# Scan and output projection of a two-block forward pass: the residual addition of a product group moved ahead of a scan step's outputs, and a finer wait for the split tiles

## The chip, the cores and the metric

One NeuronCore of a Trainium2 chip runs the whole program in one launch. The metric is the device time of that core in microseconds (us); the time of a kernel is the median over its runs.

## What is computed

Two blocks over one sequence of 512 tokens and width 1024, all in float32. The first block projects the input, runs a dilated window attention and a Mamba-2 scan, and joins both by one output projection:

```python
y = ssd_chunked(...)                       # 4 chunks of 128 tokens, 16 heads in 2 groups
y = y + d_skip[:, None] * xs_h
y_ssm = rms_norm(y * silu(z_ssm), ssm_norm_g)
mix = concatenate([y_att, y_ssm], axis=-1)             # 2048 columns
out = einsum('bse,ed->bsd', mix, w_out)                # 2048 x 1024 weights
x = layer_norm(alpha * x + out, ln_g, ln_b)
```

In a chunk the scan needs, for each group g of 8 heads: the products C.B (one 128x128 tile), the decay matrix of each head (an exponential of differences of sums), the masked product of both, that matrix times x*dt (y_diag), C times the running state (y_off), and the new state. The second block (a gated delta rule mixer with its own projections) follows and is not touched.

## The kernel before

The program has four phases on one core: the first projections, the attention, `scan_and_output` (from about 388 to 562 us of the span) and `second_mixer` (from there to the end). Only `scan_and_output` is concerned. Each engine has its own instruction list, written out by hand, and the lists meet only in semaphores.

**The work of the phase.** There are 8 scan steps (`STEPS`, step s is chunk s // 2 and head group s % 2). Beside them runs the output projection for the attention half of `mix`, in 8 groups (`GROUPS`). Group i makes one tile of 128 tokens by 512 columns: it sums 8 row tiles of weights, each as three products of split numbers (`three_products`, lines 129 to 131: high by high, high by low, low by high), so 24 matmuls into PSUM bank ACC (bank 7). VectorE then adds the tile, scaled by a factor of its row, to `resid` (`add`, line 1257) and increments `added`. There is only one such bank, so group i + 1 may not start before `added` has reached i + 1. The weights come in 8 units of 4 row tiles; of each unit ScalarE makes the high part (`round`, line 280) and VectorE the low part (`rest`, line 284).

**TensorE's order.** For s = 0 to 6: `ahead_of(s + 1)`, `group(s)`, `outputs(s)`; after the loop `outputs(7)` and `group(7)`. (`ahead_of(0)` and `ahead_of(1)` come before the loop.) `ahead_of` transposes the next step's inputs (L942, L949), makes C.B (L950) and the sums for the decays (L956). `outputs` makes y_off (L967), the state's part (L974) and eight y_diag products (L978); it waits for `z_ok` of the step before, since VectorE must have read the banks.

**VectorE's order.** In iteration s: `steps_of(s + 1)` (x times dt, L1203, L1207, and the masked C.B, L1214) and `masked(s + 1)` (L1220), then `outputs(s)` (L1229 to L1253; the last, L1253, increments `z_ok`), then `add_group(s)` (L1257). At s = 3 `rest(2)` stands ahead of `outputs(3)`, and `rest(3)` between `outputs(3)` and `add_group(3)`. `steps_of(0)`, `masked(0)`, `steps_of(1)` and `masked(1)` come before the loop. ScalarE's `ahead_of(s + 1)` (L1074, L1079, L1083) waits for `z_ok` of step s - 1, then copies the transposed inputs, on which the next `steps_of` waits. GpSimd makes the sums' inputs (L1146) and a skip term (L1153).

**The second half of the projection.** After group 7, TensorE transposes the first four column tiles of the scan's result (`turn`, L934); ScalarE writes each one's high part (`high`, L1067), VectorE its low part (`low`, L1194, increments `m_lo_ok`). Then come four token tiles of unit 4 in banks 4 to 7, each of 12 products. Ahead of all four stands one wait for the first four low tiles:

```python
            pe.wait_ge(w.lo_ready, 5)
            pe.wait_ge(m_lo_ok, KT + 4)
            for t in range(TT):
                if t == TT - 1:
                    pe.wait_ge(added, GROUPS)
                mm = unit_tile(4, t, 4 + t, True, False)
                if t == 1:
                    for e in range(KT + 4, MT):
                        turn(e)
```

Units 5 to 7 follow, and VectorE normalises the rows of `resid` as the token tiles are finished. The next phase starts when all engines have left this one.

Of the kernel before, what the change touches and what calls it, by code (L numbers as in the profile page):

```python
# [15 lines left out]
KT = D_MODEL // P  # L16
# [59 lines left out]
class Phase(ExitStack):  # L76
# [14 lines left out]
    def sem(self, name):  # L91
        s = self.enter_context(self.nc.semaphore(f"{self.name}_{name}"))
        Phase.used.append(s.num)
        return s
# [32 lines left out]
def three_products(nc, out, w_hi, w_lo, x_hi, x_lo, first, last):  # L127

    nc.tensor.matmul(out, w_hi, x_hi, start=first, stop=False, skip_group_check=True)  # L129
    nc.tensor.matmul(out, w_hi, x_lo, start=False, stop=False, skip_group_check=True)  # L130
    return nc.tensor.matmul(out, w_lo, x_hi, start=False, stop=last, skip_group_check=True)  # L131
# [685 lines left out]
def scan_and_output(nc, a, ahead, wba, wba_in, mix_in, raw, att_f, m_g, masks, small, resid, row_f, tok, xbc, dt, adt, modc):  # L817
# [8 lines left out]
    STEPS = G * TT  # L826
# [7 lines left out]
    with ctx:  # L834
# [35 lines left out]
        turned, m_hi_ok, m_lo_ok = sem("turned"), sem("m_hi_ok"), sem("m_lo_ok")  # L870
# [14 lines left out]
        def head_row(values):  # L885

            return values.unsqueeze(2).broadcast_to([P, HPG, HD])

        def heads_of(g):
            return slice(g * HPG, (g + 1) * HPG)  # L890
# [4 lines left out]
        def slot_of(e):  # L895

            return e % KT
# [27 lines left out]
        def _(pe):  # L925
            pe.sem_inc(w.units_used, 2)

            def turn(e):

                bank = 7 - e % 4 if e < KT else e % 4  # L930
                if e % KT >= 4:
                    pe.wait_ge(m_lo_ok, e - 3)
                for t in range(TT):
                    tr = nc.tensor.transpose(ps[:, bank, t * P:(t + 1) * P], tok[:, t, e * P:(e + 1) * P], ident)  # L934
                tr.then_inc(turned, 1)
# [42 lines left out]
                    mm = nc.tensor.matmul(ps_yd[:, h, :], E[:, g, h, :], xdt[:, g, h, :], start=True, stop=True)  # L978
                mm.then_inc(yd_made, 1)

            def unit_tile(u, t, bank, first, last):
                s, k0 = u % 2, OUT_UNITS[u][1]
                rows = slice(t * P, (t + 1) * P)
                for kk in range(HALF):
                    k = slot_of(k0 + kk)
                    mm = three_products(nc, ps[:, bank, :], m_hi[:, k, rows], m_lo[:, k, rows],
                                        w.hi[s][:, kk, :], w.lo[s][:, kk, :], first and kk == 0, last and kk == HALF - 1)
                return mm

            def group(i):  # L990
                n, t = divmod(i, TT)
                if i:
                    pe.wait_ge(added, i)
                for x in range(2):
                    u = 2 * n + x
                    pe.wait_ge(w.lo_ready, u + 1)
                    if i == 0:

                        pe.wait_ge(m_lo_ok, KT if x else HALF + 1)
                    mm = unit_tile(u, t, ACC, x == 0, x == 1)  # L1000
                    if t == TT - 1:
                        mm.then_inc(w.units_used, 1)
                    elif x:
                        mm.then_inc(acc_made, 1)

            flat = adt[:].rearrange("p c h -> p (c h)")
            for n, mask in enumerate((upper, below, ones)):
                mm = nc.tensor.matmul(ps_c[:, n, 0:TT * SSM_HEADS], mask, flat, start=True, stop=True)
# [17 lines left out]
            for e in range(KT, KT + 4):  # L1026
                turn(e)
            pe.wait_ge(w.lo_ready, 5)
            pe.wait_ge(m_lo_ok, KT + 4)
            for t in range(TT):  # L1030
                if t == TT - 1:
                    pe.wait_ge(added, GROUPS)
                mm = unit_tile(4, t, 4 + t, True, False)
                if t == 1:
                    for e in range(KT + 4, MT):
                        turn(e)
# [3 lines left out]
            for t in range(TT):  # L1040
                mm = unit_tile(5, t, 4 + t, False, True)
                if t < TT - 1:
                    mm.then_inc(acc_made, 1)
# [11 lines left out]
            for j in range(3 * KT):  # L1055
                mm = nc.tensor.matmul(ps[:, 4, j:j + P], mod_acc[:, j * P:(j + 1) * P], ones, start=True, stop=True)
# [128 lines left out]
        def _(dve):  # L1185
            own = Own(dve, own_s)

            def rest(u):
                w.rest(nc.vector, dve, u % 2, u // 2)
# [7 lines left out]
            def steps_of(s):  # L1197
                c, g = divmod(s, G)

                dve.wait_ge(xs_out, s + 1)  # L1200
                if s >= G:
                    dve.wait_ge(yd_made, s - 1)
                ins = nc.vector.tensor_tensor(xdt[:, g], ps_x, head_row(dt[:, c, heads_of(g)]), ALU.mult)  # L1203
                if s < FIRST:
                    if s >= G:
                        dve.wait_ge(st_made, s - 1)
                    ins = nc.vector.tensor_tensor(xdte[:, g], ps_x, head_row(dte[:, c, heads_of(g)]), ALU.mult)  # L1207
                ins.then_inc(x_read, 1)
                dve.wait_ge(cb_made, s + 1)
                if s < FIRST:  # L1210
                    dve.wait_ge(b_out, s + 1)
                if s >= G:
                    dve.wait_ge(m_ok, s - 1)
                nc.vector.tensor_tensor(cb[:, g, :], ps_c[:, 1, :], upper, ALU.mult).then_inc(cb_ok, 1)  # L1214

            def masked(s):
                g = s % G
                dve.wait_ge(cb_ok, s + 1)
                dve.wait_ge(e_ok, s + 1)
                nc.vector.tensor_tensor(E[:, g], E[:, g], cb[:, g, :].unsqueeze(1).broadcast_to([P, HPG, P]), ALU.mult)\  # L1220
                    .then_inc(m_ok, 1)

            def outputs(s):
                c, g = divmod(s, G)
                if s:
                    dve.wait_ge(z_ok, s)
                if c:
                    dve.wait_ge(yo_made, s - 1)
                    own.did(nc.vector.tensor_tensor(y[:], ps_yo, head_row(decays[:, 0, c, heads_of(g)]), ALU.mult))  # L1229
                    y_step = own.n  # L1230
                    if s < FIRST:
                        dve.wait_ge(st_ok, s - 1)
                        own.did(nc.vector.tensor_tensor(state[:, g], state[:, g], head_row(decays[:, 2, c, heads_of(g)]), ALU.mult))
                        state_step = own.n
                dve.wait_ge(yd_made, s + 1)
                if c:
                    own.wait(y_step)
                    own.did(nc.vector.tensor_tensor(y[:], ps_yd, y[:], ALU.add))
                    y_step = own.n
                if s < FIRST:  # L1240
                    dve.wait_ge(st_made, s + 1)
                    if c:
                        own.wait(state_step)
                        nc.vector.tensor_tensor(state[:, g], ps_st, state[:, g], ALU.add).then_inc(st_ok, 1)
                    else:
                        nc.vector.tensor_copy(state[:, g], ps_st).then_inc(st_ok, 1)
                dve.wait_ge(xskip_ok, s + 1)
                if c:
                    own.wait(y_step)
                own.did(nc.vector.tensor_tensor(y[:], y[:] if c else ps_yd, xs_tok[:, g], ALU.add))  # L1250
                z = tok[:, c, D_MODEL + g * GW:D_MODEL + (g + 1) * GW].rearrange("p (h e) -> p h e", e=HD)
                own.wait()
                nc.vector.tensor_tensor(z, y[:], z, ALU.mult).then_inc(z_ok, 1)  # L1253

            def add(half, t, bank, factor):
                x = resid[:, t, half * COLS:(half + 1) * COLS]
                nc.vector.scalar_tensor_tensor(out=x, in0=ps[:, bank, :], scalar=factor[:, t:t + 1], in1=x,  # L1257
                                               op0=ALU.mult, op1=ALU.add).then_inc(added, 1)

            def add_group(i):  # L1260
                n, t = divmod(i, TT)
                if i == 0:
                    dve.wait_ge(factor_ok, 1)
                    dve.wait_ge(rows_in, 64)
                if t < TT - 1:
                    dve.wait_ge(acc_made, (TT - 1) * n + t + 1)
                else:
                    dve.wait_ge(w.units_used, 2 + 2 * (n + 1))
                add(n, t, ACC, att_f)
# [17 lines left out]
            for s in range(STEPS):  # L1287
                if 1 <= s < STEPS - 1:
                    steps_of(s + 1)
                    masked(s + 1)  # L1290
                if s == TT - 1:
                    rest(2)
                outputs(s)
                if s == TT - 1:
                    rest(3)
                if s < STEPS - 1:
                    add_group(s)
            rest(4)
            for e in range(KT, KT + 4):
                low(e)  # L1300
# [1428 lines left out]
```

## Time and profile before

| what | value |
|---|---|
| time, median of 3 runs | 1202.41 us (1197.02 to 1203.72) |
| the profiled execution's own time | 1204.67 us |
| its span, first to last instruction | 1202.8 us |
| granted TensorE clock, mean over the span | 0.972 of full |
| TensorE matmul busy, share of the span | 93% |
| VectorE, ScalarE, GpSimd busy | 59%, 39%, 18% |

How to read it: the times of a row are in microseconds, "mean ns" is the mean length of one instruction in nanoseconds. PE is TensorE's matmuls, PEld its weight loads, which overlap them, DVE is VectorE, ACT ScalarE, POOL GpSimd; an engine name with a q is its queue. Matmuls are pipelined and their ends are modelled, so two neighbours overlap in the records. "<-" in square brackets names the work that ended an idle time. The clock is given as a fraction: 1.00 is 2.4 GHz, 0.50 is 1.2 GHz, and a number between them is a stretch with some of each.

### The profile page before, as it was taken

To read this page: it belongs to the slowest core of one execution; us is meant where nothing else is said; L and a number is where in the kernel's file an instruction comes from. 1 tells how busy PE (TensorE), PEld (TensorE's weight loads), DVE (VectorE), ACT (ScalarE), POOL (GpSimd) and SP (SyncE) were. 2 spreads that over 40 slices of the span, in tenths; PEclk is the share of its full clock that TensorE was granted. 3 is DMA by queue.
4 is the path that set the end of the run, shared out by engine and by line. 5 is a ranking of instruction groups with operands and counts; after the bars stand their busy time and mean duration, and the time that the engine had idled before them with its cause. 6 is when DMAs were issued, how large, how long until landed. Compare 5 with 4: busy or idle time off the path is not lost.

```text
span 1202.8 us, 15175 instructions
## 1 busy us (share of the span) xinstructions
PE 1123.1 (93%) x5878; PEld 930.5 (77%) x5878; DVE 705.3 (59%) x1144; ACT 465.8 (39%) x853; POOL 218.9 (18%) x155
## 2 busy tenths in 40 slices
PE   6999999999899998896999999999999889999887
PEld 3888888888698766685687888788798867788776
DVE  3344446521465875447558667566545667756778
ACT  3233134421565531222343333476244446244421
POOL 0001000000000421006100000033433233444044
PEclk9999999999899999898999999999999979999989
DMA  7277424330410410222144354432211212121401
GB/s 276 81 251 255 164 85 143 99 128 0 132 54 17 173 36 35 96 97 87 68 140 141 127 189 140 140 118 93 71 53 54 88 37 88 35 71 36 158 1 71
DMA packets 58307, 124.04 MB, mean 103 GB/s; under 512 B 5760, under 2 KB 5888, under 8 KB 58112
## 3 DMA queue, kind: packets, MB, share of 16 engines
q1 hardware_dynamic: 55792, 110.22, 27.2%
q0 software_dynamic: 2304, 12.58, 2.8%
q8 instruction: 44, 0.72, 0.2%
q10 hardware_dynamic: 144, 0.33, 0.1%
q14 instruction: 23, 0.19, 0.1%
HBM read 108.96 MB, written 14.16 MB: 102 GB/s over the span
## 4 chain that ended last, share of the span: by engine, by line
PE 39%; DVE 8%; issue 2%; POOL 2%; ACT 2%; DMA 0%; DVEq 0%; POOLq 0%; ACTq 0%
PE mixer_ps L129 8%; PE mixer_ps L130 8%; PE mixer_ps L131 8%; PE mixer_ps L1833 3%; PE mixer_ps L1831 3%; DVE z L2580 2%; PE mixer_ps L1859 2%; DVE resid L240 1%; PE mixer_ps L1873 1%; PE mixer_ps L1864 1%; PE mixer_ps L1835 1%; POOL mixer_w_lo L284 1%; PE mixer_ps L1794 1%; PE mixer_ps L1845 1%; PE mixer_ps L1805 1%
## 5 line engine op out<-in xcount | busy, mean ns | idle before, releaser
L284 DVE TENSOR_TENSOR projections_w_lo<-raw,projections_w_hi 128x2048 fp32r<-128x2048 f32 x26 | 59.6, 2293 | 146.1 <-ACT projections_w_hi L280 146.1
L280 ACT ACTIVATE projections_w_hi<-raw 128x2048 fp32r<-128x2048 f32 x26 | 49.8, 1914 | 158.8 <-PE projections_ps L131 157.2
L284 DVE TENSOR_TENSOR mixer_w_lo<-raw,mixer_w_hi 128x2048 fp32r<-128x2048 f32 x21 | 48.1, 2289 | 71.1 <-ACT mixer_w_hi L280 60.3
L129 PE MATMUL projections_ps<-projections_x_hi,projections_w_hi 128*128 128x512 f32 x224 | 87.3, 390 | 0.0
L131 PE MATMUL projections_ps<-projections_x_hi,projections_w_lo 128*128 128x512 f32 x224 | 87.1, 389 | 0.0
L130 PE MATMUL projections_ps<-projections_x_lo,projections_w_hi 128*128 128x512 f32 x224 | 87.1, 389 | 0.0
L129 PE MATMUL projections_ps<-projections_w_hi,projections_x_hi 128*128 128x512 f32 x192 | 74.7, 389 | 0.0
L130 PE MATMUL projections_ps<-projections_w_lo,projections_x_hi 128*128 128x512 f32 x192 | 74.7, 389 | 0.0
L131 PE MATMUL projections_ps<-projections_w_hi,projections_x_lo 128*128 128x512 f32 x192 | 74.7, 389 | 0.0
L240 DVE SCALAR_TENSOR_TENSOR resid<-resid,mixer_cw 128x512 f32<-128x512 f32 x96 | 64.9, 745 | 0.0
L129 PE MATMUL output_ps<-output_w_hi,output_m_hi 128*128 128x512 f32 x128 | 53.1, 415 | 9.3 <-DVE resid L1257 6.5
L129 PE MATMUL mixer_ps<-mixer_w_hi,mixer_ha_hi 128*128 128x512 f32 x128 | 55.9, 437 | 5.9 <-ACT z L2065 2.6
L2526 DVE COPY_PREDICATED mixer_space<-mixer_masks,mixer_ps 128x512 f32<-128x512 int32 x48 | 35.4, 737 | 43.4 <-PE mixer_ps L1833 42.9
L2296 POOL TENSOR_TENSOR mixer_es<-masks,mixer_gsel 128x1024 f32<-128x1024 f32 x8 | 15.5, 1939 | 230.9 <-DVE mixer_bsel L2448 197.0
L129 PE MATMUL mixer_ps<-mixer_w_hi,mixer_hb_hi 128*128 128x512 f32 x128 | 52.1, 407 | 1.5 <-POOL mixer_w_lo L1548 1.4
L130 PE MATMUL output_ps<-output_w_lo,output_m_hi 128*128 128x512 f32 x128 | 51.8, 404 | 0.0
L280 ACT ACTIVATE mixer_w_hi<-raw 128x2048 fp32r<-128x2048 f32 x18 | 34.3, 1908 | 44.5 <-PE mixer_ps L131 44.5
L131 PE MATMUL output_ps<-output_w_hi,output_m_lo 128*128 128x512 f32 x128 | 51.4, 401 | 0.0
L130 PE MATMUL mixer_ps<-mixer_w_lo,mixer_ha_hi 128*128 128x512 f32 x128 | 51.3, 401 | 0.0
L131 PE MATMUL mixer_ps<-mixer_w_hi,mixer_ha_lo 128*128 128x512 f32 x128 | 51.1, 399 | 0.0
L129 PE MATMUL mixer_ps<-mixer_ha_hi,mixer_w_hi 128*128 128x512 f32 x128 | 50.0, 391 | 0.7 <-DVE mixer_w_lo L284 0.7
L1833 PE MATMUL mixer_ps<-mixer_space 128*128 128x128 f32 x384 | 50.4, 275 | 0.0
(309 smaller groups left out, 2860.9 us busy)
## 6 DMA issues: line engine op xcount, KB each, us to landing
raw<-in_w_in SPq DMA_DIRECT2D x26, 1024.0 KB, 5.1
raw<-in_gdn_w_in SPq DMA_DIRECT2D x24, 1024.0 KB, 5.1
tok<-in_ada_w POOLq DMA_DIRECT2D x16, 768.0 KB, 6.4
raw<-in_w_out SPq DMA_DIRECT2D x8, 1024.0 KB, 5.8
qkv_kept<-mixer_ring SPq DMA_DIRECT2D x8, 1024.0 KB, 4.3
mixer_st<-qkv_kept SPq DMA_DIRECT2D x32, 256.0 KB, 3.0
raw<-in_gdn_w_out SPq DMA_DIRECT2D x8, 1024.0 KB, 5.3
resid<-in_att_bias SPq DMA_DIRECT2D x16, 256.0 KB, 2.7
```

The lines of the kernel that those rows point to most:

```text
L129: nc.tensor.matmul(out, w_hi, x_hi, start=first, stop=False, skip_group_check=True)
L130: nc.tensor.matmul(out, w_hi, x_lo, start=False, stop=False, skip_group_check=True)
L131: return nc.tensor.matmul(out, w_lo, x_hi, start=False, stop=last, skip_group_check=True)
L240: ins = nc.vector.scalar_tensor_tensor(out=acc, in0=src, scalar=tap, in1=acc, op0=ALU.mult, op1=ALU.add)
L280: self.nc.scalar.activation(self.hi[s][:], self.raw[s][:], ACT.Copy).then_inc(self.hi_ready, 1)
L284: engine.tensor_tensor(self.lo[s][:], self.raw[s][:], self.hi[s][:], ALU.subtract)\
L1831: mm = nc.tensor.matmul(out, C[:, 8 * j + m, :], T[:, m, :], start=True, stop=True)
L1833: mm = nc.tensor.matmul(out, V[:, m, :], U[j % 2][:, m, :], start=True, stop=True)
L1859: mm = nc.tensor.matmul(psW[:, h, :], U[slot][:, 4 * h + c, :], rhs, start=True, stop=True)
L2296: nc.gpsimd.tensor_tensor(steps, upper.unsqueeze(1).broadcast_to([P, 8, P]), gs.unsqueeze(2).broadcast_to([P, 8, P]), ALU.mult).then_inc(s ...
L2526: nc.vector.copy_predicated(U[j % 2][:, 4 * grp:4 * grp + 4, :], level.unsqueeze(1).broadcast_to([P, 4, P]), psZ[:, grp, :].rearrange("p ( ...
L2580: nc.vector.scalar_tensor_tensor(out=zz, in0=O[j % 2][:, h, c, :], scalar=rs[:, j % 2, h, c:c + 1], in1=zz, op0=ALU.mult, op1=ALU.mult).th ...
```

## The change

In VectorE's loop `add_group(s)` moves from behind `outputs(s)` (and behind `rest(3)` at s = 3) to ahead of `outputs(s)` (and behind `rest(2)`). In TensorE's list the one wait for four low tiles ahead of unit 4 goes, and the first token tile (t = 0) waits ahead of each of its four weight row tiles for the low tile that it needs. No arithmetic, transfer or buffer is added or removed.

```diff
-            def unit_tile(u, t, bank, first, last):
+            def unit_tile(u, t, bank, first, last, lows=False):
                 s, k0 = u % 2, OUT_UNITS[u][1]
                 rows = slice(t * P, (t + 1) * P)
                 for kk in range(HALF):
+                    if lows:
+                        pe.wait_ge(m_lo_ok, k0 + kk + 1)
                     k = slot_of(k0 + kk)
                     mm = three_products(nc, ps[:, bank, :], m_hi[:, k, rows], m_lo[:, k, rows],
                                         w.hi[s][:, kk, :], w.lo[s][:, kk, :], first and kk == 0, last and kk == HALF - 1)
...
             pe.wait_ge(w.lo_ready, 5)
-            pe.wait_ge(m_lo_ok, KT + 4)
             for t in range(TT):
                 if t == TT - 1:
                     pe.wait_ge(added, GROUPS)
-                mm = unit_tile(4, t, 4 + t, True, False)
+                mm = unit_tile(4, t, 4 + t, True, False, t == 0)
...
                 if s == TT - 1:
                     rest(2)
+                if s < STEPS - 1:
+
+                    add_group(s)
                 outputs(s)
                 if s == TT - 1:
                     rest(3)
-                if s < STEPS - 1:
-                    add_group(s)
             rest(4)
```

## Rows read from the trace of the kernel before

**Rows 1.** Waits from 402 to 562 us: in total, times, longest, in us.
```profile
PE output_ps L129 <- DVE resid L1257: 6.5, 6, 3.1
...
PE output_ps L129 <- DVE output_m_lo L1194: 2.7, 1, 2.7
...
PE output_ps L967 <- DVE tok L1253: 2.3, 1, 2.3
```
**Rows 2.** Timeline of PE, before the steps and in steps 2 to 4: start, length, line.
```profile
395.02 1.88 PE L956 MATMUL output_ps<-output_steps_in,masks 128*128 128x512 f32 x4
396.74 1.91 PE L934 MATMUL output_ps<-masks,tok 128*128 128x128 f32 x16
...
430.98 1.02 PE L967 MATMUL output_ps<-output_state,xbc 128*128 128x512 f32 x2
...
437.96 0.50 PE L129 MATMUL output_ps<-output_w_hi,output_m_hi 128*128 128x512 f32 x1 [0.87 <-DVE resid L1257]
...
443.54 1.02 PE L967 MATMUL output_ps<-output_state,xbc 128*128 128x512 f32 x2
...
447.76 1.88 PE L956 MATMUL output_ps<-output_steps_in,masks 128*128 128x512 f32 x4
452.71 0.63 PE L129 MATMUL output_ps<-output_w_hi,output_m_hi 128*128 128x512 f32 x1 [3.07 <-DVE resid L1257]
...
459.90 0.59 PE L967 MATMUL output_ps<-output_state,xbc 128*128 128x512 f32 x1
```
**Rows 3.** Timeline of DVE, steps 2 and 3.
```profile
432.11 0.69 DVE L1229 TENSOR_TENSOR output_y<-output_ps,output_decays 128x512 f32<-128x512 f32 x1 [2.67 <-PE output_ps L967]
...
436.55 0.69 DVE L1253 TENSOR_TENSOR tok<-output_y,tok 128x512 f32<-128x512 f32 x1
437.16 0.74 DVE L1257 SCALAR_TENSOR_TENSOR resid<-output_ps,att_f,resid 128x512 f32<-128x512 f32 x1
437.96 0.69 DVE L1203 TENSOR_TENSOR output_xdt<-output_ps,dt 128x512 f32<-128x512 f32 x1
...
439.49 2.51 DVE L1220 TENSOR_TENSOR output_E<-output_E,output_cb 128x1024 f32<-128x1024 f32 x1
443.02 2.29 DVE L284 TENSOR_TENSOR output_w_lo<-raw,output_w_hi 128x2048 fp32r<-128x2048 f32 x1 [1.03 <-ACT output_w_hi L280]
...
447.18 0.69 DVE L1238 TENSOR_TENSOR output_y<-output_ps,output_y 128x512 f32<-128x512 f32 x1 [0.67 <-PE output_ps L978]
...
449.71 2.28 DVE L284 TENSOR_TENSOR output_w_lo<-raw,output_w_hi 128x2048 fp32r<-128x2048 f32 x1
451.91 0.74 DVE L1257 SCALAR_TENSOR_TENSOR resid<-output_ps,att_f,resid 128x512 f32<-128x512 f32 x1
```
**Rows 4.** Timeline of ACT and POOL around steps 2 and 3.
```profile
437.34 0.60 ACT L1074 ACTIVATE output_xs_tok<-output_ps 128x512 f32<-128x512 f32 x1 [9.83 <-DVE tok L1253]
...
438.01 1.05 POOL L1153 TENSOR_TENSOR output_xs_tok<-output_xs_tok,small 128x512 f32<-128x512 f32 x1 [9.65 <-ACT output_xs_tok L1074]
...
450.56 2.33 POOL L1153 TENSOR_TENSOR output_xs_tok<-output_xs_tok,small 128x512 f32<-128x512 f32 x1 [9.65 <-ACT output_xs_tok L1074]
```
**Rows 5.** Stretches: us, busy time (x instructions) of each engine, PEclk, DMA share, GB/s.
```profile
452.70:456.20 3.50, 3.49 (x9) 2.71 (x10) 3.10 (x4) 0.00 (x0) 2.05 (x2) 0.53 0.77 277
...
490.10:494.90 4.80, 4.80 (x19) 3.92 (x19) 1.28 (x2) 0.00 (x0) 0.00 (x0) 0.54 0.43 134
...
506.10:513.30 7.20, 7.18 (x24) 5.69 (x25) 2.73 (x2) 0.31 (x1) 0.00 (x0) 0.76 0.66 240
```
**Rows 6.** Timeline of DVE and PE around the start of unit 4.
```profile
503.25 2.72 DVE L1194 SCALAR_TENSOR_TENSOR output_m_lo<-output_ps,mix_g,output_m_hi 128x512 fp32r<-128x512 f32 x4
...
501.56 1.91 PE L934 MATMUL output_ps<-masks,tok 128*128 128x128 f32 x16
506.12 0.47 PE L129 MATMUL output_ps<-output_w_hi,output_m_hi 128*128 128x512 f32 x1 [2.65 <-DVE output_m_lo L1194]
```
**Rows 7.** The second mixer as one stretch, columns as above.
```profile
562.00:1202.80 640.80, 596.14 (x3254) 501.06 (x3254) 418.92 (x676) 272.20 (x611) 166.28 (x97) 0.97 0.28 94
```

## The prediction

> **What bounds the kernel now.** I read the stretches first, then the waits, then the timeline of each engine. Over the phase TensorE has work nearly all the time, so what ends a wait of TensorE moves the end of the phase, and everything behind it. The table of waits shows three kinds that end on VectorE [rows 1]: the first product of a group waits for the residual addition (L1257) six times, 6.5 us in all, 3.1 us the longest; the first product of unit 4 waits 2.7 us for the low tiles; and the products of step 7 wait 2.3 us for step 6's result (L1253). The change aims at the first two and leaves the third.
>
> In the timeline group 3's last product is followed at 443.54 by the scan's products, and these by step 5's preparation, whose last four matmuls start at 447.76; then TensorE is idle until 452.71 [rows 2]. VectorE meanwhile works through the outputs, a weight unit's low part (449.71, 2.28 us) and only then the addition (451.91) [rows 3], although the tile was complete at about 443.5. So the addition is late only by its place in the list. For step 2 the same shape is smaller: the addition runs at 437.16, behind L1253.
>
> **The clock** belongs to the same bill. The granted clock is 0.53 in the 3.5 us behind the idle 3.1 us, 0.54 in the 4.8 us behind the idle 2.3 us, and 0.76 over the 7.2 us that follow the 2.7 us ahead of unit 4 [rows 1, 5]: stretches at the 1.2 GHz level, each behind an idle. The idle 0.87 us ahead of group 3 leaves no mark: its 24 products take 5.58 us [rows 2].
>
> **Part 1: the addition ahead of the outputs.** The wait for `added` goes if VectorE is at the addition when the group ends. Steps 1 to 6 have it so: for step 2 the group ends at 430.98 (start of L967), and VectorE is idle 2.67 us until 432.11, for L967's result [rows 2, 3]. The addition (0.74 us) fits between the tile's end, about 431.2, and 432.11, so the outputs and `z_ok` don't move. At step 3 VectorE is in `rest(2)` until 443.02 + 2.29 = 445.31 [rows 3], so the outputs start 0.7 us late; L1238 had been idle 0.67 us for TensorE and absorbs most of it. I take 0.2 us late for `rest(3)`. At step 0, whose outputs follow the first masks without a pause, nothing on VectorE covers the addition; its outputs come up to 0.74 us later, and what hides that is group 1 on TensorE, 5.6 us; without it step 1 would pay the 0.74.
>
> What is late next? TensorE's period is, group end to group end, 3.4 us of outputs, 2.5 of preparation and 5.5 of products, about 11.4. VectorE's period starts with the outputs, which end at 437.24, 6.26 us behind the group's end. Then ScalarE's copy (437.34 to 437.94) [rows 4] releases L1203 at 437.96, exactly where it starts today: the addition filled that hole and does not shorten the chain when it goes. The masked product ends at 439.49 + 2.51 = 442.00, 11.0 us behind the group's end [rows 3]. That is 0.4 us ahead of the next group's end, so VectorE just keeps up.
>
> The gain per wait: reported idle is 6.5 us over six waits [rows 1]. It counts from the modelled end of the last preparation matmul (1.88 us behind the first), while in an unbroken row the next instruction starts 1.72 us behind it (395.02 to 396.74 [rows 2]). That adds 6 x 0.16 = 1.0: **7.5 us**. Bounds: 6.5, and 7.5 if all of the pitch comes back. Group 4 also gets its clock back: it took 459.90 - 452.71 = 7.19 us, group 3 443.54 - 437.96 = 5.58 [rows 2]: **1.6 us**. The second half of group 4 needs `rest(3)`. That ended at 451.99, 8.45 us behind the group's end; group 4 would start 5.9 behind it and reach its second half at 5.9 + 2.8 = 8.7, and with 0.2 us of lateness `rest(3)` ends at 8.65 and hands over at about 8.8. I subtract **0.2** (bounds 0 and 1.0).
>
> The upper bound is where a GpSimd operation would start ahead of `rest(3)` and hold it up. The row: the GpSimd multiplication L1153 took 1.05 us at step 2 and 2.33 us at step 3, where it began at 450.56 inside `rest(3)` [rows 3, 4]. The Trainium skill, "SBUF — State Buffer", section "Who interferes with whom", says that the port which VectorE and GpSimd share is an exclusive lock: whoever starts first holds it for its whole instruction. By that rule the loser would be `rest(3)` only if L1153 came first, and the sum would be 11.7 in place of 12.5. L1153 waits for ScalarE's copy, which waits for the same L1253 that `rest(3)` follows directly, so both move together and I keep 0.2.
>
> **Part 2: a wait per low tile.** The four low tiles run from 503.25 to 505.97, so one is done each 0.66 us and the first at 503.25 + 0.74 = 503.99. TensorE started 0.15 us behind the last one (506.12) [rows 6]; now it starts at 504.14: **2.0 us**. Each row tile then takes three products at 0.23 (5.58 / 24), 0.7 us in all, as slow as the low tiles come, so no further wait. Four wait instructions come in where one was. Group 3 passes such a satisfied wait between its two units and keeps that pitch, so I cost them at zero (bounds 0 and 4 x 0.2, one exposed weight load each). Behind them on TensorE stands all of unit 4, for which ScalarE waits (rounding unit 6). Nothing is moved past the queues of SP or GpSimd; SP's loads wait for `lo_ready`, whose events hardly move. The addition of group 7, behind the low tiles, is needed only by the fourth token tile, some 8 us later.
>
> The clock: 24 products in 7.18 us [rows 5], while 24 at full clock take about 5.5: **1.6 us**, if the clock stays. What stays between group 7 and unit 4 are the 16 transposes (501.56 to 503.47) and an idle of 0.7 us instead of 2.65 [rows 6], nearer to the 0.87 us that did no harm than to the 2.3 that did. Bounds 0 and 1.6.
>
> **Sum**: 7.5 + 1.6 - 0.2 + 2.0 + 1.6 = **12.5 us**. Against the profiled execution's 1204.67 that is 1192.2. That execution stands 2.3 us above the median of the three runs, 1202.41; 1202.41 - 12.5 = 1189.9, and I give **1190.0**. The wait in front of step 7 stays: it hangs on VectorE's outputs of step 6, which move with TensorE's. The second mixer (640.8 us of the span [rows 7]) only starts earlier.
>
> **Rivals.**
> *The clock falls all the same at unit 4* or in group 4. For it: only a part of the 7.2 us behind the wait was slow (0.76 [rows 5]), so the fall is not tied to the wait alone, and small transposes come ahead of it. Against: the 0.87 us ahead of group 3 did nothing. Gain 12.5 - 1.6 = 10.9, with both 9.3: 1191.5 to 1193. Chance 0.2.
> *VectorE becomes the bound of the scan steps.* For it: the slack is only 0.4 us, and the list is in order, so a late mask now delays the addition, and with it the outputs. Against: L1229 and L1238 wait for TensorE anyway (1.1 and 0.7 us [rows 3]). Price up to 0.75 us, one addition, in each of six steps: gain 12.5 - 4.5 = 8.0, so 1194.4. Chance 0.1.
> *The waits on the addition are not what holds TensorE*: something else (the weight's low part, the next inputs) ends just behind it. Then only unit 4 gains, 2.0 to 3.6 us: about 1199.6, no change. For it: at step 3 `rest(3)` ends 0.08 us before the addition's start. Against: only the group's second half needs it, and the small waits have no such neighbour. Chance 0.08.
> *Slower: the clock's slow stretches in the second mixer grow.* The mechanism is that more of its short waits are followed by a stretch at 1.2 GHz, as the three above were, since everything there now starts 12 us earlier. One such stretch costs 1.6 us (7.19 - 5.58). It decides from 8 new stretches (12.5 / 1.6) and is slower by over 0.5% from 12: 1202.4 - 12.5 + 12 x 1.6 = 1209.1. The mixer's mean clock is 0.97 [rows 7], so it now holds 640.8 x 0.03 x 2 = 38 us at the lower level; 12 more of 3.5 us would double that. Chance 0.03.
>
> **How the numbers follow.** The forecast's case has 0.59, the clock at unit 4 or group 4 0.2, VectorE 0.1, no gain from the addition 0.08, slower 0.03. About 0.5%, 6 us, is what a measurement of this kernel can tell from no change (the three runs spread over 6.7 us). The low end takes the forecast's gain, 2.2 us more (4.8 x 0.46 [rows 5]) if the slow clock behind step 6 vanishes by the shift, and a median as far down as half of the runs' spread: 1184. The high end holds the first two rivals and most of the noise: 1198. Faster by over 0.5% is below 1196.4: 0.87; within: 0.10; slower: 0.03.
>
> **What would show it.** In the changed profile: no waits of L129 on L1257, or traces of 0.1 us; group 4 about 5.6 us long at clock 1.00; L1257 directly ahead of L1229 in VectorE's timeline and L1203 still 7.0 us behind the group's end; the wait on L1194 at about 0.7 us, with clock 1.00 behind it; the wait of 2.3 us on L1253 still there; the next phase about 12 us earlier. I would be wrong if L129 waited on L284 or L1220, if the same idle came back under another name ahead of L967, or if clock rows in the mixer fell.

## The result and the profile after

The changed kernel takes 1188.96 us (median; 1182.84 to 1190.15) against 1203.02 of the kernel before in the same comparison: ratio 0.9886, 95% interval 0.9846 to 0.9926, 14.1 us less. Measured again beside other kernels it was 1187.68 against 1202.69, ratio 0.9874 (0.9859 to 0.9889). The forecast was 1190.0, range 1184 to 1198, and 0.87 for a gain of over 0.5%.

In the changed file the lines from 990 on are one or two higher: L1257 is L1258, L1253 L1254, L1194 L1195, L1203 L1204, L1229 L1230. In some of the runs below they are shifted by one or two more (L1196 is L1194, L1255 is L1253).

The head of the page, then the waits from 402 to 550 us (in total, times, longest):

```profile
span 1188.4 us, 15175 instructions
```
```profile
DVE resid L1258 <- PE output_ps L131: 14.7, 10, 2.3
...
PE output_ps L967 <- DVE tok L1254: 2.3, 1, 2.3
...
PE output_ps L129 <- DVE output_m_lo L1195: 0.6, 1, 0.6
```

The six waits of L129 on the addition [rows 1] are gone without a trace. In their place VectorE waits for TensorE: ten waits of its additions for a finished tile, since VectorE is now there first. The wait ahead of unit 4 fell from 2.7 to 0.6 us, and the one for step 6's result is still 2.3.

TensorE's timeline, against [rows 2] and [rows 6]:

```profile
412.12 1.88 PE L956 MATMUL output_ps<-output_steps_in,masks 128*128 128x512 f32 x4
...
441.30 1.02 PE L967 MATMUL output_ps<-output_state,xbc 128*128 128x512 f32 x2
...
445.52 1.88 PE L956 MATMUL output_ps<-output_steps_in,masks 128*128 128x512 f32 x4
446.84 0.79 PE L129 MATMUL output_ps<-output_w_hi,output_m_hi 128*128 128x512 f32 x1
...
452.74 1.02 PE L967 MATMUL output_ps<-output_state,xbc 128*128 128x512 f32 x2
...
475.34 1.02 PE L967 MATMUL output_ps<-output_state,xbc 128*128 128x512 f32 x2
480.40 2.06 PE L967 MATMUL output_ps<-output_state,xbc 128*128 128x512 f32 x2 [2.31 <-DVE tok L1254]
...
493.51 1.91 PE L934 MATMUL output_ps<-masks,tok 128*128 128x128 f32 x16
496.06 0.47 PE L129 MATMUL output_ps<-output_w_hi,output_m_hi 128*128 128x512 f32 x1 [0.65 <-DVE output_m_lo L1195]
...
501.61 1.91 PE L934 MATMUL output_ps<-masks,tok 128*128 128x128 f32 x16
```

From the end of group 3 to the end of group 4 it is 452.74 - 441.30 = 11.44 us, where it was 459.90 - 443.54 = 16.36. L129 now starts inside L956's modelled length. VectorE's timeline, against [rows 3]:

```profile
430.07 0.75 DVE L1258 SCALAR_TENSOR_TENSOR resid<-output_ps,att_f,resid 128x512 f32<-128x512 f32 x1 [1.16 <-PE output_ps L131]
431.00 0.69 DVE L1230 TENSOR_TENSOR output_y<-output_ps,output_decays 128x512 f32<-128x512 f32 x1 [0.18 <-PE output_ps L967]
...
436.85 0.69 DVE L1204 TENSOR_TENSOR output_xdt<-output_ps,dt 128x512 f32<-128x512 f32 x1 [0.72 <-ACT output_xs_tok L1075]
...
447.48 2.29 DVE L284 TENSOR_TENSOR output_w_lo<-raw,output_w_hi 128x2048 fp32r<-128x2048 f32 x1
...
451.19 2.41 DVE L1221 TENSOR_TENSOR output_E<-output_E,output_cb 128x1024 f32<-128x1024 f32 x1
453.52 0.74 DVE L1258 SCALAR_TENSOR_TENSOR resid<-output_ps,att_f,resid 128x512 f32<-128x512 f32 x1
```

The addition lies in the hole ahead of L1230, and the hole that it leaves behind the outputs is now the wait of 0.72 us for ScalarE's copy. And the stretches of step 7 with group 7, and of the first two token tiles of unit 4, against [rows 5]:

```profile
480.40:485.50 5.10, 5.10 (x18) 4.07 (x19) 0.69 (x1) 0.00 (x0) 0.00 (x0) 0.50 0.35 104
485.50:493.50 8.00, 8.00 (x26) 6.34 (x26) 2.61 (x4) 1.92 (x1) 0.00 (x0) 0.68 0.32 133
...
496.00:501.60 5.60, 5.54 (x24) 4.56 (x25) 4.75 (x5) 2.38 (x2) 0.00 (x0) 1.00 0.60 187
```

**The bill of the first pair of profiles**, from TensorE's landmarks: group 6 ends 9.68 us earlier (485.02 to 475.34). Group 7 ends only 8.05 earlier (501.56 to 493.51), since step 7 and group 7 took 13.11 us at a lower clock, not 11.48. Unit 4 starts 10.06 earlier (506.12 to 496.06) and its first 24 products end 11.69 earlier (513.30 to 501.61). The second mixer's first VectorE operation moved from 562.26 to 550.57, again 11.69. The span fell by 14.4: the other 2.7 us came in the second mixer, 640.6 us from there to the end before and 637.8 after, where no instruction was changed. The granted clock of the mixer differs between the two profiles:

```profile
562.26:1202.83 640.57, 596.14 (x3254) 501.06 (x3254) 418.91 (x676) 272.20 (x611) 166.28 (x97) 0.97 0.28 94
...
550.57:1188.35 637.78, 590.80 (x3254) 496.91 (x3254) 418.87 (x676) 272.17 (x611) 167.77 (x97) 0.98 0.28 94
```

### The profile page after: what moved, and what is told of

Same layout as the page of the kernel before. It is cut to its first block, busy times and chain, and to the rows that moved or that the text cites. A ratio compares the mean times of both kernels' runs of the same rounds, so it can differ in the third digit from the quotient of the medians.

```text
span 1188.4 us, 15175 instructions
## 1 busy us (share of the span) xinstructions
PE 1115.0 (94%) x5878; PEld 926.3 (78%) x5878; DVE 706.2 (59%) x1144; ACT 465.9 (39%) x853; POOL 220.5 (19%) x155
## 4 chain that ended last, share of the span: by engine, by line
PE 37%; DVE 10%; issue 3%; ACT 2%; POOL 2%; DMA 0%; DVEq 0%; POOLq 0%; ACTq 0%
PE mixer_ps L129 7%; PE mixer_ps L131 7%; PE mixer_ps L130 7%; PE mixer_ps L1835 3%; PE mixer_ps L1833 3%; DVE z L2582 2%; PE mixer_ps L1861 2%; DVE resid L240 1%; PE mixer_ps L1875 1%; DVE resid L2660 1%; PE mixer_ps L1866 1%; PE mixer_ps L1837 1%; DVE mixer_ktok L2658 1%; POOL mixer_w_lo L284 1%; PE mixer_ps L1796 1%
## 5 line engine op out<-in xcount | busy, mean ns | idle before, releaser
L129 PE MATMUL projections_ps<-projections_x_hi,projections_w_hi 128*128 128x512 f32 x224 | 87.3, 390 | 0.0
L129 PE MATMUL projections_ps<-projections_w_hi,projections_x_hi 128*128 128x512 f32 x192 | 74.7, 389 | 0.0
L129 PE MATMUL mixer_ps<-mixer_w_hi,mixer_ha_hi 128*128 128x512 f32 x128 | 54.9, 429 | 5.9 <-ACT z L2067 2.6
L129 PE MATMUL output_ps<-output_w_hi,output_m_hi 128*128 128x512 f32 x128 | 54.1, 423 | 0.7 <-DVE output_m_lo L1195 0.6
L129 PE MATMUL mixer_ps<-mixer_w_hi,mixer_hb_hi 128*128 128x512 f32 x128 | 52.1, 407 | 1.5 <-POOL mixer_w_lo L1550 1.4
L129 PE MATMUL mixer_ps<-mixer_ha_hi,mixer_w_hi 128*128 128x512 f32 x128 | 50.0, 391 | 0.7 <-DVE mixer_w_lo L284 0.7
```

## The experiments

Theory: what goes is idle of TensorE in two independent places, with the time that the clock takes behind an idle. Rivals: VectorE's chain is or becomes the bound; the clock's part is chance; only one place counts. For comparison I use the stretch from L956 of step 2's preparation (412.11 in the kernel before, 412.12 in the changed one) to the second mixer's first VectorE operation. It leaves out the first 400 us, which differ by up to 3.4 us from profile to profile, and the mixer. It is 150.15 us before and 138.45 after; the changed kernel run again gave 138.40, but the kernel before, profiled again, gave 146.81. One profile of each is therefore not enough to compare stretches; the table further down takes the slow clock out of them.

> The changed kernel itself, beside the three below on one chip. Theory: 13 to 14 us below the kernel before; the stretch of step 7 and group 7 at the lower clock, as in its first profile, or as short as before (4.8 us less 1.6).

Measured: 15.0 us below, 1.0 more than the expectation allowed; step 7 and group 7 took 13.03 us, at the lower clock again.

**Only the additions** (the new waits taken back):

```diff
             pe.wait_ge(w.lo_ready, 5)
+            pe.wait_ge(m_lo_ok, KT + 4)
...
-                mm = unit_tile(4, t, 4 + t, True, False, t == 0)
+                mm = unit_tile(4, t, 4 + t, True, False)
```

> The changed kernel with one wait for four low tiles again, so only the additions are moved. Theory (the gain is idle of TensorE that goes, with the clock that hung on it, in two independent parts): all six waits of L129 on the addition are gone; group 4 starts near 446.8 us and takes 5.7 us; the wait ahead of unit 4 is 2.65 us again and the clock behind it below 1; the second mixer's first VectorE operation, at 562.3 in the kernel before and 550.6 in the changed one, stands at 552.6 to 554.2; time 1191 to 1195. Rival (the two parts overlap, or what was gained is a chance shift of the clock): at 550.6, or above 556.

Measured: 1190.90 us, ratio 0.9914 (0.9891 to 0.9938), 11.9 us less and just below the expected range. All six waits are gone, but the stretch was 136.95 us, shorter than with both parts. Its timeline and clock say why:

```profile
479.01 1.12 PE L967 MATMUL output_ps<-output_state,xbc 128*128 128x512 f32 x2 [2.30 <-DVE tok L1255]
...
487.23 1.91 PE L934 MATMUL output_ps<-masks,tok 128*128 128x128 f32 x16
491.79 0.77 PE L129 MATMUL output_ps<-output_w_hi,output_m_hi 128*128 128x512 f32 x1 [2.65 <-DVE output_m_lo L1196]
```
```profile
479.00:487.20 8.20, 8.19 (x42) 6.73 (x43) 3.25 (x5) 1.92 (x1) 0.00 (x0) 1.00 0.55 195
491.80:498.70 6.90, 6.90 (x24) 5.59 (x25) 2.70 (x2) 0.29 (x1) 0.00 (x0) 0.78 0.71 239
```

Step 7 and group 7 took 8.2 us at clock 1.00 behind the same idle of 2.3 us that cost 11.5 and 13.1 elsewhere. So the same idle does not always cost the clock. The first operation of the mixer, at 547.7, missed the expected 552.6 to 554.2 for this reason and because this profile runs 1.4 us ahead by step 2. Profiled again, the same kernel took 12.65 us there, and its stretch was 140.01.

**Only the finer wait** (the additions behind the outputs, as before):

```diff
-                if s < STEPS - 1:
-
-                    add_group(s)
                 outputs(s)
                 if s == TT - 1:
                     rest(3)
+                if s < STEPS - 1:
+                    add_group(s)
```

> The changed kernel with the additions behind the outputs again, so only the finer wait for the low tiles is there. Theory: six waits of L129 on the addition, 6.5 us; unit 4 starts 0.15 us behind the first low tile, 2.0 us earlier than before, with the clock at 1.00 behind it, 1.6 us; second mixer's first VectorE operation at 558.7; time 1198 to 1200. Rival (the transposes ahead, or the phase of the clock, keep the slow stretch): 560.3.

Measured: 1200.29 us, ratio 0.9983 (0.9969 to 0.9997), 0.3 us above the expected range. The wait ahead of unit 4 is 0.65 us and its 24 products take 5.58 us. The stretch is 147.65, 2.5 less than in the first profile of before: 2.0 of idle and 1.6 of clock gained at unit 4, 1.1 lost to the clock in group 4, which took 8.3 us here behind its idle. By the second profile of before (146.81) it would be 0.8 more, since that one lost less to the clock. The timed medians are 2.5 us apart.

**Only group 3's addition ahead of the outputs:**

```diff
+                if s == TT - 1:
+                    add_group(s)
                 outputs(s)
                 if s == TT - 1:
                     rest(3)
-                if s < STEPS - 1:
+                elif s < STEPS - 1:
                     add_group(s)
```

> The kernel before with only the addition of group 3 ahead of the outputs (the other six stay behind them). Theory: group 4 starts without a wait and runs at full clock: 3.2 + 1.6 us; the other five waits stay at 3.4 us in all; second mixer's first VectorE operation at 557.4 to 557.6; time 1197 to 1199. Rival (the small waits cost nothing since they hide behind VectorE's chain, so that this one move brings all of the 9.7 us that the additions brought): 552.6.

Measured: 1193.96 us, ratio 0.9935 (0.9914 to 0.9956), 8.8 us less, where 1197 to 1199 was expected; the mixer's first VectorE operation came at 554.3, not at 557.4 to 557.6. The five other waits stay, 3.4 us in all. From group 3's end to group 4's it is 11.45 us, 4.9 less than before, as in the changed kernel. The stretch is 143.61, 6.5 less; the other 1.6 is unit 4, whose products took 5.55 us at full clock behind the full wait of 2.65. With the clock left out, this move brings 3.3 of the 8.1 us that all the additions bring (table below); the five small waits cost the other 4.8. In the timed medians it is 8.8 of 11.9 us, more than that share; why is open.

**Group 3's addition ahead of rest(3), still behind the outputs:**

```diff
                 outputs(s)
-                if s == TT - 1:
-                    rest(3)
                 if s < STEPS - 1:
                     add_group(s)
+                if s == TT - 1:
+                    rest(3)
```

> The kernel before with only the addition of group 3 moved ahead of the weight unit's low part (rest(3)), still behind the outputs. Theory: group 4 starts at about 450.5, 2.2 us earlier, behind an idle of about 0.9 us, which like the other small ones does not cost the clock: 2.2 + 1.6 us; second mixer's first VectorE operation at 558.5. Rival (the clock falls by a phase of its own, not by the length of the idle): 560.1; a second rival (group 4 is really held by rest(3)): 562.3, no change.

Measured: 1198.87 us, ratio 0.9966 (0.9953 to 0.9979).

```profile
446.42 1.88 PE L956 MATMUL output_ps<-output_steps_in,masks 128*128 128x512 f32 x4
449.17 0.50 PE L129 MATMUL output_ps<-output_w_hi,output_m_hi 128*128 128x512 f32 x1 [0.87 <-DVE resid L1257]
454.79 1.02 PE L967 MATMUL output_ps<-output_state,xbc 128*128 128x512 f32 x2
```

The idle is 0.87 us, and the group takes 5.62 us. From group 3's end to group 4's it is 12.60 us, 3.8 less, by a swap with one weight operation. Group 4 wasn't held by `rest(3)`: it started as soon as the addition was done, and its second half did not wait for the low part either. The mixer's first VectorE operation came at 556.7, not 558.5; the difference is the slow stretch that unit 4 did not have here (5.55 us) and step 2 starting 1.3 us earlier in this profile, less a longer slow stretch at step 7 (12.62 us).

**Filling the waits.** Products without use, into the state's bank (free at those times), in the changed kernel's wait ahead of step 7, and in the kernel before's wait ahead of group 4 (there 13, behind `st_ok` 4):

```diff
+            pe.wait_ge(st_ok, FIRST)
+            for n in range(10):
+                nc.tensor.matmul(ps[:, ST, :], m_hi[:, n % 8, 0:P], w.hi[1][:, n % 4, :], start=True, stop=True)
             outputs(STEPS - 1)
```

> The changed kernel with ten products without use (split attention tiles by weights, into the bank of the state, which is free by then) put into TensorE's wait of 2.3 us ahead of step 7's outputs. Theory (the slow stretch behind that wait hangs on the idle): the idle is filled, outputs and group 7 run at 1.00 and take 8.1 us in place of 13.1; second mixer's first VectorE operation at 545.6; time 5 us below the changed kernel. Rival (the stretch is slow by its own phase, or since the outputs are many small matmuls): still 550.6.

> The kernel before with 13 products without use put into the wait of 3.1 us ahead of group 4. Theory (the slow stretch behind that wait hangs on the idle): group 4 starts at about the same time, at most 0.6 us late, and takes 5.5 us at clock 1.00 in place of 7.2 to 8.3. Rival (its slow stretch comes from elsewhere): 7.2 us or more again.

Step 7 and group 7: 8.24 us instead of 13.11 (479.18 to 487.42), stretch 133.64, so 4.8 us less, and 1184.35 us, ratio 0.9843 (0.9828 to 0.9859), 3.3 us below the changed kernel, where 5 was expected (the four runs end at 1185.17, those of the changed kernel begin at 1186.70): TensorE works more and the kernel is faster. Group 4 in the kernel before:

```profile
447.46 3.55 PE L1022 MATMUL output_ps<-output_w_hi,output_m_hi 128*128 128x512 f32 x13
451.10 0.50 PE L129 MATMUL output_ps<-output_w_hi,output_m_hi 128*128 128x512 f32 x1
...
456.69 1.02 PE L967 MATMUL output_ps<-output_state,xbc 128*128 128x512 f32 x2
```
```profile
451.10:456.70 5.60, 5.60 (x25) 4.62 (x26) 3.08 (x4) 0.00 (x0) 2.04 (x2) 1.00 0.62 190
```

It starts at its old place behind L956 (4.96 us against 4.95) and takes 5.59 us at clock 1.00, where three profiles with the idle gave 7.2, 8.3 and 7.1. The idle is what lets the clock fall there. In time it does not show: this kernel was timed in one execution, 1198.30 us, and the kernel before, run again beside it, in one of 1198.69 us. That one lost 3.1 us to the clock at the three places together, the filled one 3.2.

**How fixed are the slow stretches?** The kernel before and the one with only the additions, profiled again.

> The kernel before once more, for its slow stretches alone. Theory (the wait that is removed always costs its idle; what the clock takes behind it is drawn anew in each execution): group 4's wait is 3.1 us again and the group takes between 5.6 and 8.3 us; step 7 with group 7 takes between 8.2 and 13.1 us; 24 products of unit 4 take 5.6 or 7.2 us. Rival (each kernel has its own fixed slow stretches): 7.19, 11.48 and 7.18 us, as in the first profile.

> The kernel with only the additions moved, once more. In its first profile step 7 and group 7 took 8.2 us behind their idle of 2.3 us, with no slow stretch. Theory (drawn anew): between 8.2 and 13.1 us, and no slow stretch in steps 1 to 6, which have no idle. Rival (fixed by the kernel): 8.2 us.

| profile | idle, then group 4 | idle, then step 7 and group 7 | idle, then 24 products of unit 4 | stretch | stretch without the slow clock |
|---|---|---|---|---|---|
| before | 3.07, 7.19 | 2.31, 11.48 | 2.65, 7.18 | 150.15 | 143.7 |
| before again | 3.07, 7.06 | 2.31, 9.90 | 2.65, 5.53 | 146.81 | 143.7 |
| filled ahead of group 4 | filled, 5.59 | 2.31, 11.44 | 2.65, 5.53 | 146.91 | 143.7 |
| only the finer wait | 3.07, 8.31 | 2.31, 11.45 | 0.65, 5.58 | 147.65 | 141.7 |
| only group 3's addition | none | 2.31, 11.46 | 2.65, 5.55 | 143.61 | 140.4 |
| group 3's ahead of rest(3) | 0.87, 5.62 | 2.31, 12.62 | 2.64, 5.55 | 145.89 | 141.5 |
| only the additions | none | 2.30, 8.22 | 2.65, 6.94 | 136.95 | 135.6 |
| only the additions again | none | 2.31, 12.65 | 2.62, 5.55 | 140.01 | 135.6 |
| changed | none | 2.31, 13.11 | 0.65, 5.55 | 138.45 | 133.6 |
| changed again | none | 2.31, 13.03 | 0.66, 5.58 | 138.40 | 133.6 |
| one more VectorE operation | none | 2.31, 12.63 | 0.64, 5.53 | 138.53 | 134.1 |
| filled ahead of step 7 | none | filled, 8.24 | 0.68, 5.55 | 133.64 | 133.6 |

The last column takes off what each place lost to the clock: group 4's time above 5.6 us, step 7 and group 7's above 8.22, unit 4's above 5.55, which are their times at clock 1.00. The idles are the same to 0.04 us in every profile; what follows them is not. Both rivals with a fixed stretch fall: the kernel before gave 11.48 and 9.90, the other 8.22 and 12.65. None of the idles below 1 us at these places or ahead of the other groups has a slow stretch behind it.

With the clock taken off, profiles of one kernel agree to 0.1 us and the parts add up: the additions are worth 8.1 us, the finer wait 2.0, both 10.1. The clock does not add to that in the phase. The kernel before lost 6.5 and 3.1 us to it in its two profiles, the changed kernel 4.9 and 4.8: what was won behind the waits that went came back at step 7. Whether the moved additions make that stretch longer is open: with all seven moved it cost 4.9, 4.8, 4.4, 4.4 us and once nothing, otherwise 1.7 to 4.4.

The kernel before and the one with only the additions were timed in one execution each here, 1198.69 and 1190.78 us.

**One more VectorE operation per step**, of the addition's size, behind each moved addition (it computes nothing that is used):

```diff
                     add_group(s)
+                    nc.vector.scalar_tensor_tensor(out=waste[:], in0=row_b[:, 0:COLS], scalar=att_f[:, 0:1], in1=row_g[:, 0:COLS],
+                                                   op0=ALU.mult, op1=ALU.add)
```

> The changed kernel with one more VectorE operation of the addition's size (0.65 to 0.75 us, on buffers of its own) behind each of the seven moved additions. Theory (VectorE has slack: it waits for TensorE inside the outputs): at most 1.0 us is lost, all of it at step 3 where the low part of a weight unit comes first; second mixer's first VectorE operation at 550.6 to 551.6. Rival (VectorE is the bound of the scan steps by now): 0.65 us in each of seven, 555.

Measured: 1190.13 us, ratio 0.9888 (0.9857 to 0.9920); stretch 138.53. The median is 2.4 us above the changed kernel's, more than the 1.0 expected, but the four runs spread over 9.3 us, so the profile has to decide. (The mixer's first VectorE operation came at 552.4, outside the expected 550.6 to 551.6, but step 2 already stood 1.8 us later in this profile.) From step 2's L956 to the end of group 6 it took 63.80 us against 63.22 in the changed kernel, 0.58 more, of which 0.55 lies between the ends of group 3 and group 4 (11.99 against 11.44). Inside group 4 TensorE now waits for `rest(3)`, the neighbour that the prediction had feared:

```profile
PE output_ps L129 <- DVE output_w_lo L284: 0.2, 1, 0.2
```

VectorE is not the bound in any other step.

**Group 7 split around step 7's outputs:**

```diff
-            outputs(STEPS - 1)
-            group(GROUPS - 1)
+            group(GROUPS - 1, (0,))
+            outputs(STEPS - 1)
+            group(GROUPS - 1, (1,))
```

(`group` takes the units to multiply as its second argument.)

> The changed kernel with group 7 cut in two: its first unit's products ahead of step 7's outputs, its second unit's behind them. Theory: the first 2.7 us fill the wait for step 6's result, so the idle of 2.3 us and the slow stretch behind it (5.0 us) go; ahead of unit 4 the wait grows from 0.65 to about 1.2 us, as the low part of that weight unit now follows step 7's outputs directly; unit 4 starts at about 489.0 in place of 496.1, second mixer's first VectorE operation at 543.5; time 7 us below the changed kernel. Rival (clock not tied to the idle): only the idle goes, 548; a second rival (the idle comes back ahead of unit 4, at 2 us or more, with its own slow stretch): 546 to 548.

> The kernel with group 7 split, once more. Theory: the stretch from step 3's preparation to the second mixer's first VectorE operation is 131.2 us again (138.4 in the changed kernel), since no idle above 1 us is left in it to be followed by a slow stretch; time 3 to 7 us below the changed kernel's 1187.7. Rival (the first profile was a lucky one): 133 us or more.

```profile
475.52 1.02 PE L967 MATMUL output_ps<-output_state,xbc 128*128 128x512 f32 x2
...
480.91 1.02 PE L967 MATMUL output_ps<-output_state,xbc 128*128 128x512 f32 x2
...
486.31 1.91 PE L934 MATMUL output_ps<-masks,tok 128*128 128x128 f32 x16
488.92 0.47 PE L129 MATMUL output_ps<-output_w_hi,output_m_hi 128*128 128x512 f32 x1 [0.70 <-DVE output_m_lo L1196]
```

```profile
475.50:480.90 5.40, 5.40 (x31) 4.42 (x30) 3.52 (x5) 0.00 (x0) 0.00 (x0) 1.00 0.00 0
480.90:486.30 5.40, 5.40 (x31) 4.37 (x30) 3.16 (x5) 1.91 (x1) 0.00 (x0) 1.00 0.63 225
```

Measured: 1184.10 us, ratio 0.9843 (0.9829 to 0.9858), and again 1182.50, ratio 0.9831 (0.9816 to 0.9846). TensorE's wait for step 6's result is gone, and the clock is 1.00 from group 6's end to the transposes. Group 6's end to the transposes takes 10.79 us instead of 18.17. The stretch is 131.16 us in both profiles, 7.3 below the changed kernel's. Of these, 3.6 us show in the timed medians of the shared comparison (1187.68 to 1184.10), and 5.2 if the later median, of another comparison, is taken. So the landmarks came as expected and the time, 7 us below, did not: the changed kernel's two profiles both had slow stretches at the long end (13.0 and 13.1 us), and the expectation counted them in full. Without the clock the gain is 2.4 us (133.6 to 131.2). The wait ahead of unit 4 was 0.70 where 1.2 was expected. This version beats both kernels: its slowest run of the shared comparison is 1185.06, the changed kernel's fastest 1186.70.

## Why the prediction was right

**The addition ahead of the outputs.** The mechanism of this part held: the wait was there only by the addition's place in the list. Predicted 7.5 of idle, 1.6 of clock, less 0.2: 8.9 us; measured 9.68 up to the end of group 6. Two terms were mis-sized. The start of a group was costed at L956's start plus 1.72 us, read from a row in which transposes follow L956. A product starts 1.32 us behind it (group 0 did so already in the trace before: 401.16 and 402.48), and the group then takes 5.87 us and not 5.58; an unbroken step is 7.18 us from L956's start to the group's end (412.12 to 419.30, 468.16 to 475.34 in the changed profile). So each wait gave back 0.27 us beyond its reported idle, where 0.16 was written, 0.7 us over six. And the 0.2 us for rest(3) was not paid: from L956's start to group 4's end it is 7.22 us (445.52 to 452.74). At step 3 the outputs did start 0.7 us late, but L1239's old pause absorbed all of it, and rest(3) started 6.18 us behind group 3's end, where it was 6.17. It ends 8.47 us behind that end (447.48 + 2.29 - 441.30), just ahead of the second half. At step 2 L1230 and `z_ok` stand where they stood (1.13 and 5.57 us behind the group's end in both profiles), and L1204 6.98 us behind it, where 7.0 was forecast.

The estimate that VectorE just keeps up was read at step 2 and did not hold at step 3, where rest(3) stands between: the next mask (L1221) ended 12.3 us behind group 3's end, 0.9 us behind the end of group 4. The addition at 453.52 came 0.8 us behind group 4's end (452.74) because of it. The outputs absorbed that: group 5 had no wait. About half of the mask's length comes with a GpSimd instruction beside it:

```profile
410.10 1.23 DVE L1221 TENSOR_TENSOR output_E<-output_E,output_cb 128x1024 f32<-128x1024 f32 x1
...
450.63 1.90 POOL L1147 TENSOR_TENSOR output_steps_in<-masks,adt 128x1024 f32<-128x1024 f32 x1
451.19 2.41 DVE L1221 TENSOR_TENSOR output_E<-output_E,output_cb 128x1024 f32<-128x1024 f32 x1
```

It took 2.41 us beside GpSimd's L1147, which ran until 452.53, and 1.23 alone; it ended 1.07 us behind L1147. The Trainium skill, "SBUF — State Buffer", section "Who interferes with whom", says that a VectorE instruction with two SBUF inputs contends with a GpSimd instruction that reads SBUF, for a port pair that is an exclusive lock. The trace agrees, and it also bears out which of the two loses beside rest(3): rest(3) came first (447.48) and took 2.29 us, where it was 2.28 before, and GpSimd's L1154, from 448.33, took 2.33 where it takes 1.04 in the steps around.

**The wait per low tile.** Predicted 2.0 us of idle; measured 2.01 (the start of unit 4 moved 10.06 where group 7's end moved 8.05). The wait left is 0.65 where 0.7 was written, and the four wait instructions cost nothing: 24 products in 5.55 us.

**The clock at unit 4, 1.6 us.** In the first pair of profiles it came out to the digit, 7.18 to 5.55 us. But as a term of the time it was too large. The wait of 2.65 us was followed by a slow stretch in two of seven profiles, so the mean worth is about 0.4 us ((1.6 + 1.4) / 7). The step that did not hold is the inference from one profile's idle and one slow stretch behind it to a slow stretch behind every idle above 2 us. The same holds at step 7, whose slow stretch the forecast held constant: of the eleven profiles with that wait in the table, ten lost 1.7 to 4.9 us behind it and one nothing. The forecast priced that stretch at 2.2 us, from the 4.8 us that its row covers; the first profile lost 3.3 (11.48 less 8.22). At group 4, behind 3.07 us, all three profiles with the wait lost 1.5 to 2.7 us, so there the 1.6 was sound.

**The sum** of 12.5 stands against a measured 14.1, and 15.0 in the second comparison. Up to the mixer the first pair of profiles gave 11.7: 9.7 + 2.0 + 1.6, less 1.6 of a longer slow stretch at step 7. Its 10.1 us without the clock are the part that was forecast by mechanism (7.5 - 0.2 + 2.0 = 9.3), and the table shows them in both profiles of each kernel. That the total also came so close is partly luck. The 3.2 us of clock in the sum were 1.6 in the first pair, and between the second profiles of both kernels the clock took 1.7 us away. The mixer's gain was in no term: from its first VectorE operation to the end the two kernels' two profiles each take 640.6 and 639.0 us before, 637.8 and 636.4 after. That length goes with the mixer's granted clock and not with what was changed: the four profiles with 0.97 took 639.0 to 640.6 us, the ten with 0.98 636.4 to 639.1, and both groups hold kernels with and without the moved additions. I don't know whether the mixer gains anything on the mean by starting earlier; that stays open. So does 1.3 to 2.2 us of the timed gain: the mean spans of the two kernels' two profiles each are 12.8 us apart, the timed medians 14.1 and 15.0. The timed medians of the parts add up as the parts do, 11.9 for the additions and 2.5 for the finer wait.

**The rivals.** The clock fell neither in group 4 nor at unit 4 of the changed kernel, in both of its profiles; it fell longer at step 7 instead, which no rival named. VectorE as the bound falls by the extra operation: seven additions more cost 0.56 us of the stretch and not 4.5. The waits were what held TensorE: their removal alone is a ratio of 0.9914. The mixer did not slow down: its granted clock was 0.98 in both profiles of the changed kernel and 0.97 in both of the kernel before.

## What to carry to other kernels

An operation that frees a buffer for the engine that sets the time belongs in its own engine's list at the first place where its input is ready, if that place lies in a hole: here seven additions moved forward brought 0.9%, and what they delayed was absorbed by a later wait. Look also for the largest wait that is left on the bounding engine and cut independent work to its size, as with group 7. And count a slow stretch behind an idle by its mean over several profiles, not by one; to see what an edit does, take the slow stretches off first. The same kernel's stretch varied by 3.3 us between two profiles, and by less than 0.1 with its slow stretches taken off.

## What the runs showed of the hardware that was not expected

A wait of 2.3 us on TensorE was followed by 1.7 to 4.9 us of loss in ten of eleven profiles, and by none in one; a wait of 2.65 us, with transposes just ahead of it, by 1.4 to 1.6 us in two of seven; one of 3.07 us by 1.5 to 2.7 us in three of three. The wait of 2.3 us was dearer (3.4 us on the mean) than the two longer ones; what tells the three places apart was not tested. Filling it with products that nobody reads made the kernel 3.3 us faster.
